# A first pass of the expert loop without tokens on TensorE

## The reference

```python
def moe_ffn(h, w_router, b_router, w_gate_up, b_gate_up, w_down, b_down):
    ...
    logits = (hf @ w_router + b_router).astype(jnp.float32)
    top_vals, top_idx = lax.top_k(logits, TOP_K)
    gates = jax.nn.softmax(top_vals, axis=-1).astype(h.dtype)
    ...
    gu = lax.ragged_dot(xs, w_gate_up, sizes) + b_gate_up[e_sorted]
    gate = jnp.minimum(gu[:, :D_FF], SWIGLU_LIMIT)
    up = jnp.clip(gu[:, D_FF:], -SWIGLU_LIMIT, SWIGLU_LIMIT)
    act = (up + 1.0) * (gate * jax.nn.sigmoid(SWIGLU_ALPHA * gate))
    out = lax.ragged_dot(act, w_down, sizes) + b_down[e_sorted]
    out = out * gates.reshape(-1)[order][:, None]
    y = jax.ops.segment_sum(out, token_of, num_segments=n_tok)
```

## Time and profile before

| What | Value |
|---|---|
| Time, median of 3 runs | 2206.56 us (2205.54 to 2211.25) |
| Time of the profiled execution | 2206.78 us |
| Its span, first to last instruction | 2205.0 us |
| PE busy | 2078.0 us, 94% |
| DVE, ACT, POOL busy | 33%, 20%, 26% |
| Tables ready, first matmul of tile 0 | 654.4 us, 671.85 us |
| End of tile 31, the last | 2159.3 us |
| Tiles with tokens | 32 |

### The profile page before, as it was taken

One profiled execution on the slowest core, in us unless ns is written; L12 is line 12 of the kernel. 1 busy time (PEld: TensorE's weight loads), 2 busy tenths in 40 slices (PEclk: granted clock), 3 DMA queues, 4 the chain that ended last, 5 costly groups with the idle time before them and its releaser, 6 DMA issues.

```text
span 2205.0 us, 41908 instructions
## 1 busy us (share of the span) xinstructions
PE 2078.0 (94%) x15574; PEld 1883.0 (85%) x15575; DVE 738.2 (33%) x1949; ACT 443.7 (20%) x1078; POOL 563.1 (26%) x645
## 2 busy tenths in 40 slices
PE   7999999999968899999999999999999999999991
PEld 6777777745538899999999999999999999999991
DVE  1322333233443334234333333333233332343331
ACT  1333323232311111111111111111111111111110
POOL 2211111100233223322222322323223233232321
PEclk9999999999978999999999999999999999999996
DMA  7100000242517889999899999999999999999987
GB/s 251 40 10 11 10 11 1 80 131 47 145 39 228 268 281 310 313 297 304 270 305 277 310 289 298 310 284 289 301 312 318 308 272 283 321 315 319 306 284 88
DMA packets 305892, 486.97 MB, mean 221 GB/s; under 512 B 105920, under 2 KB 127200, under 8 KB 305792
## 3 DMA queue, kind: packets, MB, share of 16 engines
q1 hardware_dynamic: 247184, 437.28, 60.6%
q0 software_dynamic: 33376, 45.11, 9.9%
q10 hardware_dynamic: 25280, 3.85, 1.1%
HBM read 454.83 MB, written 35.84 MB: 223 GB/s over the span
## 4 chain that ended last, share of the span: by engine, by line
PE 91%; issue 2%; DVE 2%; ACT 1%; DMA 1%; POOL 1%; ACTq 0%; DVEq 0%; SPq 0%; POOLq 0%
PE psum L1003 43%; PE psum L1019 22%; PE psum L803 8%; PE psum L952 5%; PE psum L842 3%; PE psum L911 2%; PE psum L820 2%; PE psum L910 1%; PE psum L884 1%; PE psum L932 1%; PE psum L895 1%; DMA area<-in_w_in 1%; PE psum L982 1%; DVE area L1302 0%; DVE area L1297 0%
## 5 line engine op out<-in xcount | busy, mean ns | idle before, releaser
L1003 PE MATMUL psum<-area 128*128 128x128 f32 (+3 forms) x8192 | 980.2, 282 | 37.0 <-issue 18.9
L1003 PEld LDWEIGHTS psum<-area 128*128 128x128 f32 x8192 | 971.6, 192 | 42.4 <-issue 42.4
L1019 PE MATMUL psum<-area 128*128 128x128 f32 (+3 forms) x4096 | 496.4, 282 | 0.9
L1019 PEld LDWEIGHTS psum<-area 128*128 128x128 f32 x4096 | 484.5, 191 | 10.0 <-DVE area L1302 8.7
L1283 DVE TENSOR_SCALAR area<-psum,area 128x160 f32<-128x160 f32 x256 | 86.4, 380 | 615.6 <-PE psum L1003 615.6
L600 POOL DMA_INDIRECT sum_rows<-area x165 | 264.0, 1600 | 67.4 <-issue 40.2
L762 ACT ACTIVATE area<-area 128x320 f32<-128x320 f32 x128 | 60.4, 472 | 735.8 <-DVE area L1283 735.6
L803 PE MATMUL psum<-area 128*128 128x128 f32 x1536 | 176.8, 276 | 10.5 <-ACT area L681 4.0
L803 PEld LDWEIGHTS psum<-area 128*128 128x128 f32 x1536 | 173.3, 192 | 15.3 <-ACT area L677 5.8
L590 POOL DMA_INDIRECT area<-normed_rows,area x165 | 161.3, 977 | 61.5 <-issue 61.5
L585 POOL TENSOR_TENSOR area<-area 128x5 uint32<-128x5 uint32 x33 | 6.3, 190 | 617.4 <-DVE area L1268 590.4
(11 more groups left out here) (184 smaller groups left out, 1250.6 us busy)
## 6 DMA issues: line engine op xcount, KB each, us to landing
area<-in_w_gate_up SPq DMA_DIRECT2D x256, 1024.0 KB, 6.4
area<-in_w_down SPq DMA_DIRECT2D x128, 1024.0 KB
area<-in_w_in SPq DMA_DIRECT2D x3, 2048.0 KB, 21.5
area<-in_x SPq DMA_DIRECT2D x9, 512.0 KB, 4.0
area<-in_w_o SPq DMA_DIRECT2D x1, 4096.0 KB, 13.0
sum_rows<-area SPq DMA_DIRECT2D x32, 128.0 KB
normed_rows<-area SPq DMA_DIRECT2D x8, 512.0 KB, 3.1
out<-sum_rows SPq DMA_DIRECT2D x4, 1024.0 KB, 14.0
```

The costliest lines, as they stand in the source:

```text
L1003: ins = mm(dst, w_gu[piece][:, k, c * P:(c + 1) * P], xT[:, PART * s + k, 0:width], start=(s == 0 and k == 0 and c % 2 == 0), stop=(s == 1 ...
L1019: ins = mm(bank[4 + d // 3][:, (d % 3) * SLOTS:(d % 3) * SLOTS + width], w_dn[q][:, kk, d * P:(d + 1) * P], actT[:, 2 * q + kk, 0:width], ...
```

## The change

PE's tile loop is put into an outer loop of two passes. `passes` holds two numbers: 1, and the count of tiles. So the first pass enters the first group of six and skips the other nine; the second is the pass of before. The number of tokens comes from a new table of PE's own, `held_pe`: six zeros, then the 68 entries of `held_i`. The first pass reads the six zeros, the second starts at the seventh entry. DVE fills both: the count of tiles ahead of its wait for PE, and the zeros, the 1 and the copy of the entries behind that wait and ahead of the cast that sets `tables_ready`. No other engine's code is changed.

```diff
+        held_pe, passes = take(GROUP + TABLE).bitcast(I32), take(2).bitcast(I32)
...
-            n_tiles = pe.value_load(n_i[0:1, 0:1], min_val=1, max_val=MAX_TILES)
...
-            with expert_tiles(pe, n_tiles) as t:
-                tokens = pe.value_load(held_i[0:1, bass.ds(t, 1)])
-
-                with pe.If(tokens < 1):
-                    pe.nop()
-                with pe.Else():
-                    pe.wait_ge(xT_ready, t + 1)
...
+            with pe.Fori(0, 2) as pass_no:
+                tiles_now = pe.value_load(passes[0:1, bass.ds(pass_no, 1)], min_val=1, max_val=MAX_TILES)
+                with expert_tiles(pe, tiles_now) as t:
+                    tokens = pe.value_load(held_pe[0:1, bass.ds(pass_no * GROUP + t, 1)])
+
+                    with pe.If(tokens < 1):
+                        pe.nop()
+                    with pe.Else():
+                        pe.wait_ge(xT_ready, t + 1)
...
             V.tensor_copy(n_i, total[:, E - 1:E])
+            V.tensor_copy(passes[0:1, 1:2], total[0:1, E - 1:E])
 
             dve.wait_ge(tab_turned, 1)
             turned = bank[2][0:1, 0:3 * P].rearrange("p (c n) -> p c n", c=3)
+            V.memset(held_pe[0:1, 0:GROUP], 0)
+            V.memset(passes[0:1, 0:1], 1)
+            V.tensor_copy(held_pe[0:1, GROUP:], turned[:, 2, 0:TABLE])
             V.tensor_copy(tabs_i[0:1, :, :], turned[:, :, 0:TABLE]).then_inc(tables_ready, 1)
```

More of the change, by code:

```diff
@@ L1033, in expert_tile, with narrowest @@
                         down(m, q, width)
-            with expert_tiles(pe, n_tiles) as t:
-                tokens = pe.value_load(held_i[0:1, bass.ds(t, 1)])
-                with pe.If(tokens < 1):
-                    pe.nop()
-                with pe.Else():
-                    pe.wait_ge(xT_ready, t + 1)
-                    def narrowest(widths):
-                        if len(widths) > 1:
-                            with pe.If(tokens < widths[0] + 1):
-                                expert_tile(t, widths[0])
[L1048 to L1053, removed]
+            with pe.Fori(0, 2) as pass_no:
[6 more added lines that the diff above has]
+                        pe.wait_ge(xT_ready, t + 1)
+                        def narrowest(widths):
+                            if len(widths) > 1:
+                                with pe.If(tokens < widths[0] + 1):
+                                    expert_tile(t, widths[0])
+                                with pe.Else():
+                                    narrowest(widths[1:])
+                            else:
+                                expert_tile(t, widths[0])
+                        narrowest(WIDTHS)
         @block.vector
```

## The result

The changed kernel takes 2214.15 us (median of 6 runs, 2212.89 to 2217.67), the kernel before in the same comparison 2205.09 us. The ratio is 1.004, with a 95% interval of 1.0026 to 1.0054: slower, by 6 to 12 us. The profiled execution took 2212.89 us.

The account below looks back on a forecast made before the run. TensorE, busy 94% of the span, was taken as the bound. The pass's terms put the first matmul 6.3 us later with both stalls kept: 2206.78 + 6.3 = 2213.1, stated as 2213.0 us, range 2204 to 2217 us.

Parts of the forecast that it names:

- Both stalls stay, the pass is pure cost: Likeliest case, 69%: PE's stops of 5.5 and 5.0 us before tiles 1 and 2 remain, the pass adds 6.3 us.
- The long branches at 720.2 and 772.7 us, and the 38 packets: Signs: L1048 branches over 5,000 ns before tiles 1 and 2; queue q8 one or two packets above 36.
- code run into in order displaces what was reached by a jump: Instruction memory: tile 0's, then tile 1's code displaces the loop's end, so both stalls stay.
- Its picture of tile 0: Tile 0 runs through its own 1.5 instruction packets, displacing the loop's end before jumping there.
- The cost ahead of tile 0: Tile 0's first matmul at 678.1 us instead of 671.85, 6.3 us later.
- The first fetch: First empty turn's branch to the loop's end: 5.2 instead of 0.17 us, +5.0, within 1 us either way.
- the branch of over 5 us that I named as a sign: Sign in the new profile: a branch of over 5 us near 657 us, in the first pass.
- the tables: VectorE's two memsets and cast ahead of the releasing cast: 0.35 us later, bounds 0.2 and 0.7.
- an empty turn: Each first-pass turn without tokens on PE's sequencer: 1.2 us, five between first and sixth load.
- The openings, the skips and the way back: Opening 1.4 us plus 0.2, sixth load through nine skips 7.9, back edge 0.3, second opening 1.2.
- The low clock after the stops: Low-clock stretches after PE's two stops: 2.4 and 1.6 us; 1.5 us either way if one falls otherwise.
- code stays once fetched: Rival, 12%: fetched code remains, so the pass removes both stalls, worth 7.6 and 6.5 us, giving 2198.9 us.

Follow-up runs that it names:

- depth 2: Kernel before plus a first pass of one turn that jumps via the second and third widths' code to the loop's end: ratio 0.9995, no difference.
- e8: The changed kernel with two empty passes in place of one: 2229.74 us, ratio 1.0109 to the kernel before.
- e7: Kernel before with the four widths' code in opposite order, widest first, and the wait for rows inside each: ratio 1.0008.
- e2: Kernel before plus a first pass of one turn that jumps via the second width's code to the loop's end: ratio 1.0027.
- e4: Kernel before plus a first pass of one turn that walks through the heads of all four widths' code to the loop's end: ratio 0.9992.
- e10: The changed kernel measured again beside the kernel before, no edit: 2214.88 us, ratio 1.0034.
- e5: Kernel before with a walk over all four widths' code as one extra turn ahead of tile 0, no passes: 2195.51 us, ratio 0.995.
- e6: Kernel before with that extra walking turn, started on its own semaphore before the tables are ready: 2193.31 us, ratio 0.9942.
- e1: Kernel before plus a first pass of one turn, jumping straight from the loop's head to its end, rows awaited inside each width's code: ratio 1.0032.
- e9: Kernel before with only VectorE's four new instructions filling the two tables, PE's loop unchanged: ratio 0.9997.

## Why the prediction was right

**Both stalls stay, the pass is pure cost: right, and shown.** The long branches at 720.2 and 772.7 us, and the 38 packets, are what was foretold. The reason, that code run into in order displaces what was reached by a jump, was an inference from the order of packets. The four depths bear it out: with more of the code brought before it, the loop's end survives tile 0 (depth 2), then tile 1 as well (depth 3), while thirty visits to it (e8) don't help, and in e7 two heads reached by jumps were gone again after one tile. That much is shown: whether the loop's end is still there depends on what was brought before it. That packets brought in order are put over it remains a reading, since the trace has no addresses of packets. Its picture of tile 0 was probably too small by one packet (e2), and why packets still came behind the walk in e4 is open.

**The cost ahead of tile 0: 6.3 us foretold, 5.55 measured (5.86 in e10).** Two terms were mis-sized. The first fetch cost 3.4 us and not 5.2, outside the 1 us that I had allowed it; the branch of over 5 us that I named as a sign did not come. And the tables cost 0.1 us and not 0.35. VectorE's timeline shows why, since the three new instructions behind the wait begin almost together and the last cast 0.14 us after them:

```profile
653.26 0.21 DVE L1260 CAST area<-psum 1x68 int32<-1x68 f32 x1 [1.45 <-issue]
653.26 0.06 DVE L1258 MEMSET area<- 1x6 int32 x1
653.27 0.06 DVE L1259 MEMSET area<- 1x1 int32 x1
653.40 0.35 DVE L1261 CAST area<-psum 1x204 int32<-1x204 f32 x1
```

Against that, an empty turn took 1.33 us and not 1.2 (loads from 655.6 to 665.5: 3.2 more for the fetch than for a branch without one, the rest for five turns). The openings, the skips and the way back took some 0.6 us more than their terms.

**A step that was missing: the real turns.** I wrote of the turn that it has "the same instructions as before" and gave it no cost. The count was right and the duration wrong: +2.3 us over 28 joints. The low clock after the stops moved by up to 1.5 us from one execution to the next, as the bounds had it, and in the first profile it gave back 1.5 us. So the sum of the three stretches, +6.6 us, lies so near the 6.3 foretold partly by luck: the pass cost 0.75 less, the joints 2.3 more, and the stretch with the stops 1.3 less than the prediction's terms. That the pass is pure cost was reasoned; that the sum came out to a few tenths was not.

In medians the loss was 9.1 us and, in e10, 6.8 (by the ratios 8.8 and 7.5), with overlapping intervals; the three stretches account for 6.6 and 8.0. What the first comparison has beyond that stays within its interval and is not explained, nor is it explained that it fell beyond the border of 0.3% and not on it.

**The rival "code stays once fetched"** needed what the change did not do: to bring the code in its order. When that is done, it gives 14.1 us (e4) in tiles 0 to 3, as priced (7.6 + 6.5), and 11 to 13 us in the end (e5, e6).

## What to carry to other kernels

When a branch takes microseconds, look for the instruction packet inside it, and ask what else is brought between two visits: here visiting the target early kept nothing, and bringing the code in the order in which it lies did. Time a warm-up against the wait that is to hide it, with every loop level that it passes through (here nine skipped groups were a third of it). And count the duration of register work in a loop's turn, not only the instructions: at a joint that nothing covers, a tenth of a microsecond is paid in every turn.

## What the runs showed of the hardware

- A branch to code not yet brought took 3.0 to 3.8 us in most cases of the walks, but 4.2 to 5.5 in one or two of each walk with more than one such branch (e4: 3,771, 3,272, 4,965, 3,319 ns), and 5.7 and 3.9 at tile 1 of e7. In the stalls at the ends of tiles it was always over 5 us. What makes the difference is open.
- When a packet was on its way during the first transfer of the token list, that transfer took longer. POOL waited for it 3.60 us in the kernel before and 3.59 to 3.71 in e1 to e4 and e9, where none came until its last 0.3 us; 4.54 to 4.93 in the changed kernel, e5, e7, e8 and e10, with one packet; 5.85 in e6, with two. That the packets cause it fits all twelve profiles, but no run changed this alone.
- Two memsets and a cast that follow one wait on VectorE began within 0.01 us of one another (653.26, 653.26 and 653.27).
